# MLP down: a third pair of blocks by seven products, its weight sums partly by accumulating transfers

## What is computed

```python
u = jax.nn.relu(rms_norm(h, mlp_norm_g) @ w_up)      # 256 x 8192
h = h + (u * u) @ w_down                             # w_down: 8192 x 2048
```

## Time and profile before

| | us |
|---|---|
| median of three runs | 2496.78 (2496.45 to 2496.8) |
| the profiled execution | 2497.42 |
| its span, first to last instruction | 2495.6 |
| TensorE busy | 2476.8 (99%) |
| VectorE busy | 1752.0 (70%) |
| ScalarE busy | 1258.2 (50%) |
| GpSimd busy | 29.5 (1%) |
| quads jobs | seven, the first from 548.76 on, the last ending near 1111 |

### The profile page before, as it was taken

The page is one execution under the profiler, slowest core; times in us unless marked ns, Lnnn a source line. Parts: engine busy times, 40 slices in busy tenths (PEclk is TensorE's granted clock), DMA queues, the critical chain, the costliest instruction groups (busy, mean ns, idle before and its releaser), DMA issues.

```text
span 2495.6 us, 38061 instructions
## 1 busy us (share of the span) xinstructions
PE 2476.8 (99%) x15416; PEld 2116.1 (85%) x15416; DVE 1752.0 (70%) x1978; ACT 1258.2 (50%) x1506; POOL 29.5 (1%) x26
## 2 busy tenths in 40 slices
PE   9999999999999999999999999999999999999998
PEld 7888888888888888888888888887888888888886
DVE  6656765668668577675777777775777666777777
ACT  7654344545444444445454545454654444444553
POOL 0000000000000000000000000000000000000000
PEclk9999999999999999999999999999999999999999
DMA  9454545546646546565545454555465555556553
GB/s 382 155 189 152 170 157 190 177 162 226 196 169 226 193 171 217 178 211 169 187 154 185 154 185 154 185 185 194 145 216 189 187 193 191 184 190 201 185 188 127
DMA packets 128240, 465.98 MB, mean 187 GB/s; under 512 B 14369, under 2 KB 14625, under 8 KB 127169
## 3 DMA queue, kind: packets, MB, share of 16 engines
q1 hardware_dynamic: 127920, 463.53, 55.1%
q10 hardware_dynamic: 144, 0.02, 0.0%
HBM read 461.39 MB, written 2.10 MB: 186 GB/s over the span
## 4 chain that ended last, share of the span: by engine, by line
PE 96%; issue 3%; DVE 1%; DMA 0%; ACT 0%; SPq 0%; DVEq 0%; POOL 0%; POOLq 0%
PE job L971 31%; PE job L983 16%; PE job L939 11%; PE job L940 11%; PE job L941 11%; PE job L958 2%; PE job L959 2%; PE job L960 2%; PE att L958 2%; PE att L960 2%; PE att L959 2%; PE att L1178 1%; PE att L999 0%; PE att L1011 0%; PE att L1120 0%
## 5 line engine op out<-in xcount | busy, mean ns | idle before, releaser
L1275 ACT ACTIVATE w_high<-raw 128x1024 fp32r<-128x1024 f32 (+1 forms) x883 | 919.8, 1050 | 728.4 <-PE job L941 288.5
L1594 DVE TENSOR_TENSOR w_low<-raw,w_high 128x1024 fp32r<-128x1024 f32 (+1 forms) x883 | 1045.4, 1213 | 303.9 <-ACT w_high L1275 225.9
L971 PE MATMUL job<-actA,w_high 128*128 128x512 f32 x3328 | 799.3, 392 | 0.0
L971 PEld LDWEIGHTS job<-actA,w_high 128*128 128x128 f32 x3328 | 612.8, 189 | 119.5
L983 PEld LDWEIGHTS job<-actA,w_low 128*128 128x128 f32 x3328 | 426.7, 191 | 16.2
L983 PE MATMUL job<-actA,w_low 128*128 128x256 f32 x3328 | 431.7, 283 | 0.0
L1797 DVE TENSOR_TENSOR slots<-job,slots 128x512 f32<-128x512 f32 x102 | 70.5, 691 | 344.0 <-ACT slots L1467 343.3
L939 PE MATMUL job<-w_high,actB 128*128 128x512 f32 x736 | 287.9, 391 | 2.2 <-DVE w_low L1594 1.6
L940 PE MATMUL job<-w_low,actB 128*128 128x512 f32 x736 | 286.5, 389 | 0.0
L941 PE MATMUL job<-w_high,actB 128*128 128x512 f32 x736 | 286.4, 389 | 0.0
L939 PE MATMUL job<-w_high,actA 128*128 128x512 f32 x576 | 230.9, 401 | 0.0
(11 more groups left out here) (257 smaller groups left out, 1906.1 us busy)
## 6 DMA issues: line engine op xcount, KB each, us to landing
raw<-in_weights SPq DMA_DIRECT2D x855, 512.0 KB, 4.2
M<-in_mem_t SPq DMA_DIRECT2D x8, 256.0 KB, 7.9
slots<-in_mem SPq DMA_DIRECT2D x2, 1024.0 KB, 12.2
M<-in_x_t SPq DMA_DIRECT2D x4, 512.0 KB, 13.6
H<-in_x SPq DMA_DIRECT2D x2, 1024.0 KB, 9.0
out<-H SPq DMA_DIRECT2D x8, 256.0 KB, 3.2
slots<-in_w_small SPq DMA_DIRECT2D x1, 1024.0 KB, 10.3
slots<-in_post_mix_g SPq DMA_DIRECT2D x1, 1024.0 KB, 4.8
```

The lines of the kernel that those rows point to most:

```text
L971: mm = nc.tensor.matmul(J[job.buf][:, x, :], w_high[:, w % AHEAD, cols], act_both[job.act][:, c, :, :].rearrange("p a t -> p (a t)"), star ...
L1275: nc.scalar.activation(w_high[:, s % AHEAD, cols], raw[:, s % RAW_SLOTS, cols], ACT.Copy)\
L1594: nc.vector.tensor_tensor(w_low[:, s % AHEAD, cols], raw[:, s % RAW_SLOTS, cols], w_high[:, s % AHEAD, cols].bitcast(F32), ALU.subtract).t ...
```

## The change

Three of the eight pairs of rows are sevens. The job has 5 x 8 + 3 x 7 = 61 block products, in 22 windows; the program has 898. The order alternates eights and sevens. The signs of the combinations are changed so that each is a plain sum: t3 = b12 + b22, t1 = b11 + b12, t2 = t1 + b22, t4 = t2 + b21. The first two are not made by VectorE: the seven's third window is loaded too, with b11, and GpSimd issues two transfers from HBM that add b22 onto b12 and b12 onto b11 where they lie in `raw`. GpSimd waits for the load of each slot first, and for the previous seven's two; ScalarE's split of the seven's second window and VectorE's two sums wait for both (`blocks_added`). The forms of the activations come in two parts, of which the second (`more_forms`, `more_both`) is for the third pair. ScalarE copies P5 too, and the job behind waits for the new event `sevens_read`, which comes behind the second of VectorE's eight operations. The last `u_split` comes two windows later.

```diff
-QUAD_ORDER = (("eight", 2), ("seven", 0), ("eight", 3), ("eight", 4), ("seven", 1), ("eight", 5), ("eight", 6), ("eight", 7))
+QUAD_ORDER = (("eight", 3), ("seven", 0), ("eight", 4), ("seven", 1), ("eight", 5), ("seven", 2), ("eight", 6), ("eight", 7))
...
-    "add_sevens": dict(p_copied=1, h_added=1),
+    "add_sevens": dict(p_copied=1, sevens_read=1, h_added=1),
...
-            p.put(job.end + 1 + 2 * behind, "u_split", j)
-            if j == 0:
-                p.put(job.end + 2, "u_forms", b)
+            p.put(job.end + 1 + 3 * behind - behind // 3, "u_split", j)
+            if j < 2:
+                p.put(job.end + 2, "u_forms", b, j)
...
+def added_ahead():
+
+    at = {}
+    for s in range(PLAN.windows):
+        if part_of(s) == 2:
+            at.setdefault(s - AHEAD - 4, []).append(s)
+    return at
...
             def load(w):
-                if not LOADED[w]:
+                if part_of(w) == 3:
                     return
                 if w >= RAW_SLOTS:
 
                     sp.wait_ge(low_ready, w - RAW_SLOTS + 1 + (part_of(w - RAW_SLOTS) == 0))
+                if part_of(w) == 2:
+                    sp.dma_start(raw[:, w % RAW_SLOTS, 0:COLS], d["weights"][LOAD_AT[w - 2] - 1][:, 0:COLS])\
+                        .then_inc(raw_loaded[w % RAW_SLOTS], 16)
+                    return
...
+            def split(w, s):
+
+                if part_of(s) != 2:
+                    return
+                right = d["weights"][LOAD_AT[s - 1] - 1]
+                if SUMS[s] > 1:
+                    pool.wait_ge(blocks_added, 32 * (SUMS[s] - 1))
+                pool.wait_ge(raw_loaded[(s - 1) % RAW_SLOTS], 16 * SLOT_LOADS[s - 1])
+                nc.gpsimd.dma_start(raw[:, (s - 1) % RAW_SLOTS, 0:COLS], right[:, COLS:2 * COLS], accum_op=ALU.add)\
+                    .then_inc(blocks_added, 16)
+                pool.wait_ge(raw_loaded[s % RAW_SLOTS], 16 * SLOT_LOADS[s])
+                nc.gpsimd.dma_start(raw[:, s % RAW_SLOTS, 0:COLS], right[:, 0:COLS], accum_op=ALU.add)\
+                    .then_inc(blocks_added, 16)
+            walk(n, lambda w: None, split, stage, added_ahead())
...
                 if k == 0 and job in BEHIND_QUADS:
-                    once("h_added", ADDED[BEHIND_QUADS[job], "add_sevens"])
+                    once("sevens_read", ADDED[BEHIND_QUADS[job], "add_sevens"])
...
+                elif part_of(s) == 1:
+                    act.wait_ge(blocks_added, 32 * SUMS[s])
...
-                    nc.scalar.activation(p1, quad_bank(buf, ("P", 1)), ACT.Copy).then_inc(S["p_copied"], 1)
+                    nc.scalar.activation(p1, quad_bank(buf, ("P", 1)), ACT.Copy)
+                    nc.scalar.activation(p5, quad_bank(buf, ("P", 5)), ACT.Copy).then_inc(S["p_copied"], 1)
...
-                dve.wait_ge(raw_loaded[s % RAW_SLOTS], 16 * SLOT_LOADS[s])
+                dve.wait_ge(blocks_added, 32 * SUMS[s])
                 dve.wait_ge(low_ready, s + 3 - RAW_SLOTS)
-                done(nc.vector.tensor_tensor(t1, b12, b11, ALU.subtract))
-                done(nc.vector.tensor_tensor(t2, b22, t1, ALU.subtract))
-                nc.vector.tensor_tensor(t3, b22, b12, ALU.subtract)
-                nc.vector.tensor_tensor(t4, b21, t2, ALU.subtract).then_inc(sums_made, 1)
+                done(nc.vector.tensor_tensor(t2, t1, b22, ALU.add))
+                nc.vector.tensor_tensor(t4, t2, b21, ALU.add).then_inc(sums_made, 1)
```

More of the change, by code:

```diff
@@ L502 @@
 LOAD_AT = list(itertools.accumulate(map(int, LOADED)))
-SLOT_LOADS = [sum(LOADED[w % RAW_SLOTS:w + 1:RAW_SLOTS]) for w in range(PLAN.windows)]
 def part_of(w):
@@ L512 @@
 SUMS = list(itertools.accumulate(int(part_of(w) == 1) for w in range(PLAN.windows)))
+SLOT_LOADS = [sum(LOADED[x] or part_of(x) == 2 for x in range(w % RAW_SLOTS, w + 1, RAW_SLOTS))
+              for w in range(PLAN.windows)]
 WIDE = list(itertools.accumulate(int(j.kind == "features") for j, k in WINDOW))
@@ L595, in stage @@
         if name in ("add_sevens", "add_quads"):
-            at[WINDOW[w][0], name] = counts.at("h_added", 1)
+            at[WINDOW[w][0], name] = counts.at("sevens_read" if name == "add_sevens" else "h_added", 1)
     walk(counts, lambda w: None, lambda w, s: None, stage)
@@ L693, in build, with form_of @@
         forms, forms_high, forms_low = m_slot(0), forms_both[:, 0, :], forms_both[:, 1, :]
-        form_at = lambda f, p: slice(((f - 1) * 2 + SEVENS.index(p)) * P, ((f - 1) * 2 + SEVENS.index(p) + 1) * P)
-        p1, u_one, u_two = slots[:, 4, 0:COLS], slots[:, 4, COLS:2 * COLS], slots[:, 5, 0:COLS]
+        more_forms = m_slot(1)[:, 0:COLS]
+        more_high, more_low = more_both[:, 0, :], more_both[:, 1, :]
+        def form_of(part, f, p):
+            if p < 2:
+                at = ((f - 1) * 2 + p) * P
+                return (forms_high, forms_low)[part][:, at:at + P]
+            return (more_high, more_low)[part][:, (f - 1) * P:f * P]
+        p1, u_one, u_two, p5 = (slots[:, 4 + i // 2, i % 2 * COLS:(i % 2 + 1) * COLS] for i in range(4))
         z_conv, y_gate, y_value, y_sig, y = a_slot(0), a_slot(1), a_slot(2), a_slot(3), a_slot(4)
@@ L893, in first_of @@
                 if k == 0 and job in BEHIND_QUADS:
-                    once("h_added", ADDED[BEHIND_QUADS[job], "add_sevens"])
+                    once("sevens_read", ADDED[BEHIND_QUADS[job], "add_sevens"])
                 if job.kind == "quads" and k == 0 and job in PREVIOUS_QUADS:
-                    once("h_added", ADDED[PREVIOUS_QUADS[job], "add_sevens"])
+                    once("sevens_read", ADDED[PREVIOUS_QUADS[job], "add_sevens"])
                 if job.kind == "quads" and part_of(w) == 0:
@@ L954, in quads @@
                     else:
-                        once("forms_low", job.needs[1] + 1)
-                        ah, al = (a[:, form_at(i, where)] for a in (forms_high, forms_low))
+                        once("forms_low", 2 * job.needs[1] + 1 + where // 2)
+                        ah, al = (form_of(part, i, where) for part in (0, 1))
                     to = quad_bank(job.buf, bank)
@@ L1890, in stage @@
                     wait(dve, n, "forms_high", 0)
[L1891 removed]
+                    raw_forms, high, low = ((forms, forms_high, forms_low), (more_forms, more_high, more_low))[a[1]]
+                    q = 2 - a[1]
+                    u = a_slot(2 + a[1])[:, 0:q * COLS].rearrange("p (q c x t) -> p q c x t", q=q, c=2, x=TT)
                     a11, a12, a21, a22 = (u[:, :, c, x, :] for x, c in ((0, 0), (0, 1), (1, 0), (1, 1)))
[L1893 to L1895 removed]
+                    s1, s2, s3, s4 = (raw_forms[:, i * q * P:(i + 1) * q * P].rearrange("p (q t) -> p q t", q=q)
+                                      for i in range(4))
+                    done(nc.vector.tensor_tensor(s1, a22, a21, ALU.subtract))
+                    done(nc.vector.tensor_tensor(s2, s1, a11, ALU.add))
                     nc.vector.tensor_tensor(s3, a11, a21, ALU.subtract)
@@ L1899, in stage @@
                     wait(dve, n, "forms_high")
-                    nc.vector.tensor_tensor(forms_low, forms, forms_high.bitcast(F32), ALU.subtract)\
+                    nc.vector.tensor_tensor(low, raw_forms, high.bitcast(F32), ALU.subtract)\
                         .then_inc(S["forms_low"], 1)
```

30 lines of the change are left out of this document (13 added, 17 removed).

## The result

The changed kernel took **2566.09 us** (median of 4 runs, 2563.09 to 2566.67) against 2496.67 us of the kernel before on the same chip: 1.0275 times the time, interval 1.0262 to 1.0288. It is 69 us slower, 71 us above the forecast and far outside its range.

A forecast was written before the change was run, and what follows sets the result against it. TensorE, busy 99% of 2495.6 us at full clock, was taken as the bound: 4.8 us of products saved less 2.9 of stalls, net -1.9, from 2496.78 to 2494.9 us; range 2491.5 to 2512.

The forecast's parts named there:

- TensorE's saving: Seven quads jobs, each with 61 instead of 62 combinations of three products: 4.8 us less on TensorE.
- The first lead: Quads job, window 3: time from its low split's end to its first product, claimed 2.8 us, 0.3 before the change.
- The stalls of the loop: TensorE waits where low split, loads, second accumulation, sums and next low split close over six windows: 2.9 us in all.
- What A is: Step sizing GpSimd's accumulation in the loop: taken as 3.9 us, between a lone load's 3.3 and a second-in-line's 4.4.
- A: The second accumulation's time from its release to its landing, in the six-window loop of the quads jobs: 3.9 us.
- 14A - 51.75: Sum in us of TensorE's stalls over the seven quads jobs, for A above 3.9.
- The second rival: Accumulations served in turns with the burst of loads: A = 5 gives 2510 us, 5.85 gives 2522; chance 0.32.
- the loads ahead of it: Loads between a low split's end and the second accumulation's release in the loop: claimed to take 5.1 us.
- change of the lead: Each six-window turn changes the time between low split and first product by 2.5 - A us.
- break-even: Each stall counts only where positive; the summed formula with its factor 14 holds for A above 3.9.
- 0.6 us to spare: Between the end of the add of the quads, 595.78, and the next job's first seven, 596.39, before the change.
- VectorE's 20.4 us of queue: VectorE's splits, sums and adds behind window 15, run without a pause, against TensorE's 19.7 us to the next job's first seven.

The follow-up runs named there:

- e1: The changed kernel without GpSimd's 42 accumulating transfers, leaving terms out of the sums (serves only to measure): 2492.41 us, 0.9982 of the kernel before.
- e6: The changed kernel with only t1 made by an accumulation; VectorE adds t3 in place: 2540.14 us, 1.0177 of the kernel before.
- e7: The changed kernel with SyncE issuing the first load behind a seven only when both accumulations have landed: 2545.97 us, 1.0201 of the kernel before.
- e2: The changed kernel with GpSimd's transfers as plain copies instead of accumulations (computes something else): 2529.52 us, 1.0129 of the kernel before.
- e3: The changed kernel with the order and two sevens of the kernel before, accumulations kept: 2520.97 us, 1.0097 of the kernel before.
- e9: e3 with the add of the quads moved before the next job's first sums: 2517.78 us, 1.0080 of the kernel before.
- e11: The changed kernel with only the add of the quads moved before the next job's first sums: 2562.58 us, 1.0261 of the kernel before.
- e5: The changed kernel with accumulated sums in buffers of their own, filled by GpSimd's copy and accumulation from HBM: 2494.51 us, 0.9991 of the kernel before.

## Why the prediction was wrong, and where it was right

**Right.** The place and the chain. TensorE's saving is 4.8 us (e1). The first lead was given as 2.8 us; it is 2.84. The stalls of the loop come at windows 9 and 15, in 12 of the 14 places, released by w_low, with VectorE idle ahead of its first sum, and the first seven of a pair doesn't stall. VectorE's and ScalarE's added work and the up products cost nothing (e1).

**Wrong: the step "What A is", 3.9 us.** It was bounded from above by 5.85, the third load of a burst. The two of the first job took 8.11 and 5.55, and the mean in the loop is 6.07: the value taken was low by 2.2 us, and 6 of the 14 lie above the bound. The rows that I scaled from were loads of SyncE. The reason given for the bound, that an accumulation reads as many bytes as a 512 KB load, counts bytes; it leaves out that two of them run side by side (worth 1.5 us by e6), that loads run beside them (0.8 by e7), and that for the same bytes an accumulation holds the engines longer than a copy (e2). At A = 6.07 the prediction's own formula, 14A - 51.75, gives 33 us of stalls and a time of 2525. The second rival had the mechanism and the sign; it gave 2522 at its worst.

**Wrong: the loads ahead of it.** The prediction put 5.1 us between a low split's end and the release of the second accumulation. For the two turns in the first job, piece by piece:

| piece | predicted | window 3 to 9 | window 9 to 15 |
|---|---|---|---|
| low split's end to the second accumulation's issue | 5.1 | 552.58 to 558.30, 5.72 | 568.97 to 575.31, 6.34 |
| accumulation | 3.9 | to 566.41, 8.11 | to 580.86, 5.55 |
| two sums and the low split | 2.6 | to 568.97, 2.56 | to 583.41, 2.55 |
| turn | 11.6 | 16.39 | 14.44 |
| change of the lead, TensorE's 10.2 less the turn | -1.4 | -6.2 | -4.2 |

The first row is low by 0.6 and 1.2 us. First, the prediction's own sum has a slip of 0.35 us: the second load was issued 0.38 us behind the first and came 4.4 after that, 4.8 from the split, so the load behind it was due at 5.4 and not at 5.1. (With 5.4 the stalls at A = 3.9 are some 7 us, and the forecast is 2499, still in the range.) Second, the chain hung the load of window 10 on the low split of window 3. By the wait in `load` it hangs on that of window 4: it is issued at 553.83 and 570.21, 1.25 us behind the end of window 3's and of window 9's, and lands 4.0 and 4.8 us later. And GpSimd, which is issuing the other accumulation just then (from 557.75 and 574.38 on), issues this one 0.5 and 0.3 us behind that landing.

Check for the first turn: lead 2.84 + 10.2 - 16.39 = -3.35, and TensorE stood idle 3.24. Over all 14 turns the first row has a mean of 7.0 us, 1.9 too much, and in e2 6.5, 1.4 too much, with copies of 4.5 in the mean. With both pieces the formula gives 14 x (6.07 + 1.86) - 51.75 = 59 us for the change, where 48.4 were waited, and 14 x (4.50 + 1.43) - 51.75 = 31 for e2, where 23.3 were. That is 11 and 8 too much, and 28 between the two where 25 were measured. That the slow products behind a stall make the next one shorter, as below, accounts for a part of what is too much; the rest is open. So the mechanism is right, and these two sizes turned 2.9 us of stalls into some 50: past its break-even the formula multiplies each tenth of a microsecond by 14.

One turn stands apart. In the third job the second accumulation is issued at 756.18, 12.0 us behind the split and 0.3 behind the landing of the first:

```profile
756.18 0.88 POOL L889 DMA_DIRECT2D raw<-in_weights  x1 [5.71 <-issue]
```

GpSimd had been idle for 5.71 us with no wait that the profile shows, against what the part on the change says of its queue, and TensorE's longest wait for a low split, 5.2 us, follows. In e3, e7, e9 and e11 the same accumulation, that of the eighth seven, is held for 4.4, 3.3, 4.6 and 5.5 us, in e2 and e5 it isn't. The reason stays open.

**Missing: the clock.** The prediction priced no change of it, as TensorE had never been idle here. The busy time for the same products rose by 25.6 us, and the rows show it only behind stalls, at half rate: behind 11 of the 15 waits. It isn't simply added to the waits, though. After window 9 TensorE's six windows took 14.4 - 2.35 = 12.1 us instead of 10.2, and its stall at window 15 was shorter by as much: the time from stall to stall is given by the turn of the chain, and the slow products lie inside it. Behind the last stall of a job no turn covers them. How the 69 us would split without the clock's fall can't be tried here and stays open.

**Missing: the add of the quads behind the sums.** The prediction gave this place 0.6 us to spare and counted VectorE's 20.4 us of queue as one "without a pause". It has a pause: the next job's first sums, which wait for an accumulation, stand ahead of the add. VectorE is idle there for 0.75, 4.18 and 4.78 us, and TensorE's waits for the add are 10.8 us in three places. The prediction had no term for this accumulation; it called those of the first seven hidden, which is so in the first job of a pair alone. e9 and e11 show what its place is worth: most of the wait comes back at the next window, for the accumulation is late anyhow.

The range ended at A = 5.1. What speaks from the page alone for a wider one: A had no row at all, its bound came from another engine's transfers, and the factor was 14.

## What to carry to other kernels

A transfer that adds onto loaded data makes two DMAs in series out of one. Before costing it, draw the loop: what frees the slot, what then is loaded, what is added, who splits it. If the loop closes over fewer windows than its latencies fill, every turn is late, and the error of one latency is multiplied by the number of turns; give the sums buffers of their own, so that their start hangs on nothing that the consumer has only just freed, and even slower transfers cost next to nothing (e5: accumulations of 6.4 and 8.5 us in the median, 1.9 us of waits). And look at what stands in a queue behind the instruction that now waits: work that is ready goes ahead of it.

## What the runs showed of the hardware

- **The clock after a stall.** Behind TensorE's idle times of 3.24, 2.35 and 4.12 us, its products went from 0.23 to 0.43 us apart, which is 1.2 for 2.4 GHz; behind the first of these 1.3 us after it went on, for about 3.3 us. Behind idle times of 1.57 and 1.93 us (e2), and of 1.17 in the change, the granted clock stayed at 1.00. The length of the idle time alone doesn't decide: in e2 it fell behind 1.94 us too (at 1125.2), and in the change it stayed at 1.00 behind 2.87 and 3.15 (at 957.2 and 1026.1). A fall cost 1.5 us (16 products in 5.14 us instead of 3.63) to 2.4 us (12 in 5.16 instead of 2.72). In the change this is 25.6 us of busy time, behind 11 of 15 waits. The Trainium skill (TensorE: Matmul & The Clock Gate, What's actually happening) has two states of this gate, at 1.2 and 2.4 GHz, and nothing between. The rows agree: but for one or two at a change, the products are 0.23 or 0.43 us apart, and the 0.67 and 0.93 of the stretches are means over both.
- **The accumulating transfer.** 256 KB added onto SBUF from HBM took 3.6 to 3.9 us where little else ran, and the second of two 3.8 to 8.1 in the loop; the plain copy of GpSimd took 2.8 at its shortest, 3.6 in the median. For the same 11.01 MB the accumulations made 6048 packets and the copies 3360, and held the 16 engines 2.6% and 1.2% of the span. GpSimd is held 0.88 to 1.26 us by the issue of an accumulation, and about 0.55 by that of a copy. The Trainium skill's fit (DMA: Bandwidth & Descriptors, Anatomy of one DMA) gives an estimate of 2.6 us for a transfer of 256 KB by GpSimd. The shortest copies (2.8) come near it, the accumulations don't; the measured times decide. The Trainium skill (the same page, Issuing engines are not separate DMA queues) also says that transfers of all issuing engines run on the same 16 engines. e7 agrees: with SyncE's loads held back, the median of the accumulations fell from 5.3 to 4.3 us.
- **Room on the DMA system.** e5 keeps it busy 0.76 and 0.91 of the time in the first two quads jobs, against 0.55 and 0.66 before, and TensorE's only wait there is the 0.7 us for the add of the quads.
